# Grouped attention: who multiplies the exponentials by the inverse sums, and when GpSimd makes the low weights behind it

## The reference, cut to what matters

```
h = rmsnorm_2(x, norm1_g[l]) * (1.0 + sc1) + sh1
q, k, v, u_pool = split(h @ w_in[l])
q = apply_axial_rope(rmsnorm_2(q, q_norm_g[l]), tables)
k = apply_axial_rope(rmsnorm_2(k, k_norm_g[l]), tables)
def one_block(qblk):                                    # blocked_gqa
    s = jnp.einsum('bqkgd,bskd->bkgqs', qblk, k)
    p = jax.nn.softmax(s, axis=-1)
    return jnp.einsum('bkgqs,bskd->bqkgd', p, v)
pool = pool_mixer(u_pool, w_pool[l], pool_scale[l])     # window means of 2, 4, 8, 16
mix = jnp.concatenate([att, pool], axis=-1) @ w_out[l]
x = x + g1 * mix
```

## Time and profile before

| | us |
|---|---|
| median of 3 runs | 1369.57 (1369.32 to 1369.78) |
| the profiled execution, its own time | 1370.58 |
| its span, first to last instruction | 1368.8 |
| TensorE busy in it | 1346.6 (98%) |
| VectorE, ScalarE, GpSimd busy | 676.3, 627.3, 614.2 |
| grouped attention, first scores to the first matmul of the out projection | 890.35 to 952.76 |

### The profile page before, as it was taken

One profiled execution on the slowest core, in us unless ns is written; L12 is line 12 of the kernel. 1 busy time (PEld: TensorE's weight loads), 2 busy tenths in 40 slices (PEclk: granted clock), 3 DMA queues, 4 the chain that ended last, 5 costly groups with the idle time before them and its releaser, 6 DMA issues.

```text
span 1368.8 us, 17272 instructions
## 1 busy us (share of the span) xinstructions
PE 1346.6 (98%) x6502; PEld 1086.7 (79%) x6502; DVE 676.3 (49%) x1014; ACT 627.3 (46%) x875; POOL 614.2 (45%) x448
## 2 busy tenths in 40 slices
PE   9999999999999999999999999988999999999999
PEld 7887967878877888888888887854878888888887
DVE  5445957738352543434443327587265555463111
ACT  5555256654364434343431224687244545544211
POOL 3454323445413465555555453402435555555452
PEclk9999999999999999999999999999999999999999
DMA  7223131232201243344345523101313222224422
GB/s 273 93 92 112 72 124 63 92 108 93 108 31 62 108 154 138 138 139 166 139 175 212 211 93 135 65 32 35 119 62 114 90 103 92 92 92 146 177 93 92
DMA packets 29216, 155.24 MB, mean 113 GB/s; under 512 B 3056, under 2 KB 4464, under 8 KB 14960
## 3 DMA queue, kind: packets, MB, share of 16 engines
q1 hardware_dynamic: 29168, 154.57, 31.6%
HBM read 152.46 MB, written 2.10 MB: 113 GB/s over the span
## 4 chain that ended last, share of the span: by engine, by line
issue 38%; PE 31%; POOL 26%; DVE 4%; DMA 0%; POOLq 0%; SPq 0%; ACT 0%
POOL wlo L432 26%; PE lin L1462 10%; PE lin L1464 10%; PE lin L1463 10%; DVE small L1122 1%; DVE expd L1135 1%; DMA raw<-w_slabs 0%; PE lin L1742 0%; DVE xl L974 0%; PE lin L1544 0%; PE lin L1545 0%; PE lin L1549 0%; DVE win L1339 0%; PE c_act L1518 0%; DVE small L1128 0%
## 5 line engine op out<-in xcount | busy, mean ns | idle before, releaser
L432 POOL TENSOR_TENSOR wlo<-raw,whi 128x512 fp32r<-128x512 f32 x444 | 614.0, 1414 | 739.2 <-ACT whi L459 480.2
L1462 PE MATMUL lin<-xh,whi 128*128 128x512 f32 x1000 | 391.6, 392 | 0.2 <-DVE wlo L981 0.2
L1464 PE MATMUL lin<-xh,wlo 128*128 128x512 f32 x1000 | 389.3, 389 | 0.0
L1463 PE MATMUL lin<-xl,whi 128*128 128x512 f32 x1000 | 389.1, 389 | 0.0
L459 ACT ACTIVATE whi<-raw 128x2048 fp32r<-128x2048 f32 x66 | 126.7, 1919 | 230.0 <-PE lin L1464 224.5
L1462 PEld LDWEIGHTS lin<-xh,whi 128*128 128x128 f32 x1000 | 187.7, 188 | 43.8 <-issue 4.6
L1464 PEld LDWEIGHTS lin<-xh,wlo 128*128 128x128 f32 x1000 | 187.7, 188 | 39.1
L1463 PEld LDWEIGHTS lin<-xl,whi 128*128 128x128 f32 x1000 | 187.7, 188 | 38.9 <-issue 0.2
L1462 PE MATMUL lin<-fh,whi 128*128 128x512 f32 x352 | 137.0, 389 | 0.0
L1463 PE MATMUL lin<-fl,whi 128*128 128x512 f32 x352 | 136.9, 389 | 0.0
L1464 PE MATMUL lin<-fh,wlo 128*128 128x512 f32 x352 | 136.9, 389 | 0.0
(11 more groups left out here) (364 smaller groups left out, 2045.4 us busy)
## 6 DMA issues: line engine op xcount, KB each, us to landing
raw<-w_slabs SPq DMA_DIRECT2D x111, 1024.0 KB, 4.7
adar<-ada SPq DMA_DIRECT2D x48, 512.0 KB, 5.5
decay<-decay SPq DMA_DIRECT2D x4, 512.0 KB, 8.0
h<-x_t SPq DMA_DIRECT2D x3, 512.0 KB, 6.3
out_t<-h SPq DMA_DIRECT2D x3, 512.0 KB, 8.1
rope<-rope SPq DMA_DIRECT2D x2, 512.0 KB, 7.2
memx<-mem_t SPq DMA_DIRECT2D x1, 1024.0 KB, 5.9
adar<-c_row SPq DMA_DIRECT2D x2, 512.0 KB, 4.6
```

The costliest lines, as they stand in the source:

```text
L432: return nc.gpsimd.tensor_tensor(wlo[s][:, ks, :], raw[s][:, ks, :], f(whi[s][:, ks, :]), ALU.subtract)
L1462: nc.tensor.matmul(out, whi_, xhi_, start=first, stop=False)
L1463: nc.tensor.matmul(out, whi_, xlo_, start=False, stop=False)
L1464: return nc.tensor.matmul(out, wlo_, xhi_, start=False, stop=last)
```

## The change

VectorE no longer scales the exponentials in the grouped attention (`scaled_elsewhere=True`). It makes the reciprocals and raises a new semaphore, `qkn["inverse"]`, on the reciprocal itself. It doesn't wait for its own reciprocal any more. GpSimd's code is cut in three: its loop of low weights up to slab 73, then 32 scalings of 128x512, each of which waits for the reciprocal of its step and raises `norm`, then the loop again from slab 74 on. So the low weights of slab 74 come behind the last scaling. The forgetting attention and the cross attention keep their scalings on VectorE. `ret` loses an unused semaphore.

```diff
--- before.py
+++ after.py
@@ -298,14 +298,14 @@
         ff = sems("ff", "hi lo mm ab explog sums fh minus")
         rope = sems("rope", "copy out")
         foxn = sems("foxn", "sq stat var sd out")
-        ret = sems("ret", "gate scores mul pv ev cent sq var sd g y hi lo")
+        ret = sems("ret", "gate scores mul pv ev cent sq var sd y hi lo")
         ATT = "scores negmax exp norm tp pt pv hi lo"
         fox = sems("fox", ATT)
         xat = sems("xat", ATT)
         gqa = sems("gqa", ATT)
         xkn = sems("xkn", "stat var sd out vsd vscale hi lo")
         xqn = sems("xqn", "sq stat var sd")
-        qkn = sems("qkn", "sq cp stat sd k out hi lo")
+        qkn = sems("qkn", "sq cp stat sd k out hi lo inverse")
         ffn = sems("ffn", "g act y hi lo")
         ffn2 = sems("glu2", "pc cv tap act f hi lo")
         ada = sems("ada", "act acc mod")
@@ -438,13 +438,21 @@
             for q in range(1, 4):
                 last = low_quarter(1, q)
             last.then_inc(wlo_ready, 1)
-            with pool_e.Fori(1, SLABS // 2) as i:
-                for s in range(2):
-
-                    pool_e.wait_ge(whi_ready, i * 2 + (s + 1))
-                    for q in range(4):
-                        last = low_quarter(s, q)
-                    last.then_inc(wlo_ready, 1)
+            def low_pairs(first, last_pair):
+                with pool_e.Fori(first, last_pair) as i:
+                    for s in range(2):
+
+                        pool_e.wait_ge(whi_ready, i * 2 + (s + 1))
+                        for q in range(4):
+                            last = low_quarter(s, q)
+                        last.then_inc(wlo_ready, 1)
+
+            low_pairs(1, SLAB0["out2"] // 2)
+            for n in range(32):
+                pool_e.wait_ge(qkn["inverse"], n // 2 + 1)
+                row = expd[n % 4][:, :]
+                nc.gpsimd.tensor_scalar(row, row, ring(n // 2, "inverse")[:, n % 2:n % 2 + 1], None, ALU.mult).then_inc(gqa["norm"], 1)
+            low_pairs(SLAB0["out2"] // 2, SLABS // 2)
 
 
         @block.scalar
@@ -1110,7 +1118,7 @@
             link(nc.vector.tensor_scalar(rstd[:, 0:M], lin[3][:, 0:M], EPS, EPS * EPS, ALU.mult, ALU.add))
             nc.vector.reciprocal(mem_scale, mem_scale).then_inc(xkn["vscale"], 1)
 
-            def softmax_dve(a, steps, group, width, scaled, lo_out, extra=None, late=1, added=None):
+            def softmax_dve(a, steps, group, width, scaled, lo_out, extra=None, late=1, added=None, scaled_elsewhere=False):
 
                 for j in range(steps + 2):
                     if j < steps:
@@ -1129,8 +1137,12 @@
                         last.then_inc(a["negmax"], 1)
                     if 1 <= j <= steps:
                         dve.wait_ge(a["exp"], 2 * j)
-                        link(nc.vector.reciprocal(ring(j - 1, "inverse"), ring(j - 1, "sum")))
-                        for e in range(2):
+                        inverse = nc.vector.reciprocal(ring(j - 1, "inverse"), ring(j - 1, "sum"))
+                        if scaled_elsewhere:
+                            inverse.then_inc(qkn["inverse"], 1)
+                        else:
+                            link(inverse)
+                        for e in range(0 if scaled_elsewhere else 2):
                             row = expd[(2 * (j - 1) + e) % 4][:, 0:width(j - 1)]
                             nc.vector.tensor_scalar(row, row, ring(j - 1, "inverse")[:, e:e + 1], None, ALU.mult
                                                     ).then_inc(a["norm"], 1)
@@ -1408,7 +1420,7 @@
                 dve.wait_ge(gqa["hi"], c + 1)
                 nc.vector.tensor_tensor(xl[:, c, :], lin[c % 2][:, :], f(xh[:, c, :]), ALU.subtract).then_inc(gqa["lo"], 1)
 
-            softmax_dve(gqa, 16, 4, lambda j: T, True, gqa_lo, beside_gqa_dve, late=2)
+            softmax_dve(gqa, 16, 4, lambda j: T, True, gqa_lo, beside_gqa_dve, late=2, scaled_elsewhere=True)
             residual("out2", norms["norm2"], scale=lambda k: mod[:, 2 * KT + k:2 * KT + k + 1])
             finish_norm("norm2", lambda k: mod[:, 4 * KT + k:4 * KT + k + 1], xhi, xlo, shift=3 * KT)
```

## The result

| | before | after |
|---|---|---|
| median of 9 runs | 1369.57 (1368.93 to 1371.22) | 1373.6 (1372.47 to 1374.87) |
| the profiled execution, its own time | 1370.58 | 1374.82 |
| its span | 1368.8 | 1373.0 |
| grouped attention, first scores to the out projection | 62.41 | 67.76 |

The change makes the kernel slower: ratio 1.0028, interval 1.0020 to 1.0036, 4.0 us (0.3%) between the medians. The forecast was 1366.2, in a range of 1364.6 to 1371.8.

What follows compares the result with a forecast made beforehand. VectorE was taken to set the pace where TensorE doesn't, 3.13 us per step against 2.93. Terms 0.9 - 3.9 - 0.7 + 0.3 = -3.4 took the median from 1369.57 to 1366.2, range 1364.6 to 1371.8.

Steps and rivals of the forecast that it cites:

- t: Time of one 128x512 scaling on GpSimd, without a row in the trace; taken as 0.8 us, range 0.44 to 1.67.
- The upper bound, 1.67: Limit for one GpSimd scaling: its subtraction of the same size beside VectorE, 6.66/4 = 1.67 us.
- 1 fill: First six steps of grouped attention, 890.35 to 907.18: no value products cover the longer chain; +0.9 us.
- 2 middle: Three steps of grouped attention, 907.18 to 915.96: TensorE's pace before and after; 0.
- 3 steps 9 to 15: Six steps, 915.96 to 939.07: 23.11 us falls to 19.2, from 17.6 plus 0.9 for ScalarE plus 0.7 for waits; -3.9.
- 4 wait at the end: End of grouped attention, 939.07 to 952.76: the wait of 0.80 at 943.88 goes; -0.7 us.
- 5 low weights late: Slab 74's low weights, made behind the last scaling, are ready with only 0.5 us of cover before the out projection; +0.3.
- 3.6 + 2t for two steps: Loop through exponentials, reciprocal, GpSimd's scalings and transposes: 5.2 us at 0.8, against TensorE's 5.86 for two steps.
- The collision: At 923.00 slab 74's subtractions on GpSimd make VectorE's operations 2.8 us longer together; the change removes this.
- Rival D: Slab 74's low weights come late and TensorE stands at the out projection by 1 to 2 us; 1367 to 1368.5, chance 0.09.
- Rival C: Common exclusion of VectorE and GpSimd: long scalings meet the next bias and delay the steps; +2.8 to +6, chance 0.15.
- The clock: A longer fill can move or repeat a TensorE stretch granted 0.50; one costs about 1 us, counted in the range.

Runs made afterwards that it cites:

- e4_probe: Kernel before, with groups of GpSimd operations on idle tiles added behind its end to time each form; a 128x512 scaling by a column alone took 1.56 us.
- e2_narrow: The whole change, but GpSimd scales only 256 of the 512 columns of each row; 1364.99 against 1369.51 before, ratio 0.9965.
- e10_late_bc: The whole change with scalings as broadcast products, on GpSimd only from step 4, VectorE scaling earlier steps; 1367.54 against 1369.95 before, ratio 0.9982.
- 384 columns: The whole change, but GpSimd scales only 384 of the 512 columns of each row; 1369.05 against 1369.53 before, ratio 0.9994.
- e1_order: Kernel before, all scalings still on VectorE, but slab 74's low weights wait on GpSimd for the last scaling; 1367.25 against 1369.51 before, ratio 0.9982.
- e5: The whole change, with GpSimd's 32 scalings written as products with a broadcast column; 1367.48 against 1369.53 before, ratio 0.9983.
- e3_split: The change with scalings split: VectorE scales each step's first head, GpSimd the second behind it; 1368.38 against 1369.51 before, ratio 0.9989.
- the split with the broadcast: The change with VectorE scaling the first head and GpSimd the second, as a broadcast product; 1365.84 against 1369.53 before, ratio 0.9971.

## Why the prediction was wrong

The step that failed is the size of t: "If reading sets GpSimd's pace, t is near 1.26/2 = 0.63 plus something for the scalar operand and fixed cost. I take 0.8". Reading doesn't set the pace. One input costs 1.56, two cost 1.26, and one with a broadcast column 1.04 (e4_probe). The upper bound, 1.67, held the value; the choice between the bounds was an argument on inputs that no row bore out. So the prediction's own first sign of being wrong, a mean above 1.1 on POOL, came with 1.63; its two others, biases of 0.5 and a wait for `wlo`, did not.

The terms, with e2_narrow (0.92 alone per scaling, nearest to the 0.8 taken) and after beside them:

| term | forecast | e2_narrow | after |
|---|---|---|---|
| 1 fill | +0.9 | +0.44 | +4.17 |
| 2 middle | 0 | -0.01 | +1.15 |
| 3 steps 9 to 15 | -3.9 | -4.42 | -0.70 |
| 4 wait at the end | -0.7 | -0.70 | +0.73 |
| 5 low weights late | +0.3 | 0 | 0 |

So with a scaling of about the taken length the terms come out near the prediction's, each within 0.6 and none on the side of the loss: -4.7 together for -3.4. In item 3, 1.6 us were put on top of six times 2.93, and 1.1 were there. The 0.9 in it for ScalarE was more than its own working gives (24 against 23.4). At the true length, by term:

1. *Fill.* No value products cover two scalings of 1.56; +4.17. Some of it is the half clock's, of which the fill has 3.4 us more than before: at most 1.7 by an estimate from the granted 0.50, if TensorE never waited in them, and it did wait. A stretch as long cost 0.69 in e10_late_bc's comparison.
2. *Middle and 9 to 15.* The loop, "3.6 + 2t for two steps", gives 6.87 at 1.63, and 6.84 was measured. The text missed a second bound: GpSimd has four scalings per two steps, 4 x 1.64 and 0.28 of idle time, which is 6.85. In after the two agree. At 384 columns they don't, and the loop is right: 3.6 + 2 x 1.335 = 6.27, measured 6.20 in the middle, with GpSimd's four operations at 5.67. GpSimd's own load passes TensorE's 2.93 only at 1.46 per scaling. From 1.34 to 1.63 the steps 9 to 15 lose 3.0 us, from 1.19 to 1.34 only 0.24. It fits that the second bound has come in there, but after's stretch at 937 lies there too.
3. *The collision.* Right: gone, and worth -2.85 in the six steps where it lay (e1_order).
4. *End.* The wait of 0.80 for VectorE went, two idle times for POOL came, 0.33 and 0.83; +0.73 where -0.7 was forecast.
5. *Low weights.* The last scaling ended 9.1 us after the last scores began (forecast 7.5 at 0.8, so 9.2 at 1.63), the subtractions took 5.0. They were done at 957.8, and the value products' end let the out projection start at 958.14: 3.59 us behind the products' start, as before (3.58). The cover of 0.3 us held because both sides moved. Rival D did not occur. SP loaded slab 76 at 957.94 instead of 928.51 (forecast 949), and what follows took no longer.

"Above t = 1.1 each further 0.1 costs 1.2 to 1.6 us": the slope is right, but the medians show no break there. By scalings in the kernel, with the stretches against before:

| run | mean us of a scaling | median against before | fill | middle | 9 to 15 | end |
|---|---|---|---|---|---|---|
| 256 columns | 1.03 | -4.5 | +0.44 | -0.01 | -4.42 | -0.70 |
| broadcast | 1.19 | -2.1 | +0.80 | +0.51 | -3.94 | -0.06 |
| 384 columns | 1.34 | -0.5 | +1.69 | +0.60 | -3.70 | -0.06 |
| after | 1.63 | +4.0 | +4.17 | +1.15 | -0.70 | +0.73 |

8.5 us over 0.61 is 1.4 us per 0.1, with steps of 1.5, 1.1 and 1.6 per 0.1: nearly a line from the start. The middle alone has the break, between 1.03 and 1.19; the fill answers to t at once, and that hides it in the sum. The sums of the prediction for known t were too high by some 2 us: -2.5 at 0.95, where 0.92 alone (256 columns) gave -4.5; +1.5 at 1.26, where 1.24 alone (384 columns) gave -0.5; and its +5 at 1.45 with its slope is over +6 at 1.56, where +4.0 was measured. So even with the price known the forecast would have been some 2 us off, on the slow side. A zero lies near 1.37 as a mean in the kernel.

Rival C had the sign and the time (+2.8 to +6), not the mechanism; that its time came true is luck. Its sum doesn't give that time either: ten meetings of 0.5 against 4.6 are +0.4. "If the pair of scalings is so long that the next bias meets it": ten of the 16 biases did run inside a scaling, and all 16 took 0.16; each of the ten began 0.8 us or more behind the scaling's start. Biases were held where GpSimd ran the broadcast product (up to 0.91 in e5, 0.56 in e10), and those versions are faster than after. That the two engines "exclude each other for operations of these forms" is more than after's trace shows. There they hold each other for part of a scaling only: four of the pool mixer's operations (917.72, 929.39, 934.21, 946.60), begun 0.07 to 0.16 us behind its start, took 1.07 to 1.16 for some 0.69, those begun 0.8 or more behind it no longer than alone, and the one at 943.59 (`xl<-lin,xh`), begun 0.14 behind it, took 0.69; and a window operation begun 0.18 before a scaling cost it 0.38 (e3_split). The sum of it was 2.3 us on GpSimd's scalings in after, and some of that is off the path.

The clock took about 1 us at a place, as the range allowed: 0.69 and 1.1 per stretch of 3.4 us.

What stays open: how the +4.17 of the fill splits between the longer chain and the half clock, since no run took the stretch away and left the rest as it was; by how much the queue of GpSimd itself, beside the chain, slows the steps 9 to 15; and whether the split with the broadcast is surely better than the order alone.

## What to carry to other kernels

When work moves to another engine and the trace has no row for that operation there, the whole forecast is that one price: put the operation behind the kernel's end, in the forms that would do (scaling, two tensors, broadcast), before arguing from the number of its inputs. Then check both bounds, the new engine's own load per step (2 x 1.63 against 2.93) and the chain through it: at 384 columns the load still fitted and the chain already cost time. And take a change with two halves apart: here the order was worth -2.3 and the moved work on top of it +6.3, and the best version kept the first and gave GpSimd half of the second, in its cheaper form.

## What the hardware showed that I had not expected

- On GpSimd, at 128x512 in float32: scaling by a column 1.56 us, by a constant 1.49, product of two tensors 1.26, product with a broadcast column 1.04, copy 0.61. The scaling costs 50% more than the broadcast product that computes the same.
- How GpSimd and VectorE hold each other hangs on the moment of the start and on the operation. Four of the pool mixer's operations on VectorE, begun 0.07 to 0.16 us behind the start of a column scaling, lost 0.38 to 0.49 us in after, those begun 0.8 us or more behind it nothing, nor did `xl<-lin,xh`, begun 0.14 behind it (0.69). In a steady row of both (e4_probe) a scaling took 1.85 for 1.56, and VectorE's products 0.70 and 1.06 by turns. The broadcast product held a small bias begun 0.5 us behind its start (0.56 for 0.16, e10_late_bc).
- A stretch of 3.4 us at half clock cost about 1.1 us in the normalization (four traces with it, eight without) and 0.69 in the fill (before against e10_late_bc). Useless matmuls before the first transposes gave nothing back: 1374.47 with and 1373.60 without, 1367.00 with and 1365.84 without.
